# RWKV chunk: scaled k and b stored dense and multiplied by quadrants; one idle product in each of the first eight steps of the prompt's attention

## What is computed

```python
s = jnp.einsum('bhtr,bsr->bhts', q_lat, c) + jnp.einsum('bhtp,bsp->bhts', q_rope, kr)
p = jax.nn.softmax(masked(s * SOFTMAX_SCALE), axis=-1)
return jnp.einsum('bhts,bsr->bthr', p, c)
```

```python
sa = jnp.einsum('bhij,bhj->bhi', S, -kk_t)
S = S * w_t[:, :, None, :] + sa[..., None] * (kk_t * a_t)[:, :, None, :] + v_t[..., None] * k_t[:, :, None, :]
y_t = jnp.einsum('bhij,bhj->bhi', S, r_t)
```

## Time and profile before

| | |
|---|---|
| Median of 3 runs | 2264.63 us |
| The profiled execution's own time | 2272.78 us |
| Its span, first to last instruction | 2271.1 us |
| Mean granted TensorE clock over the span | 0.935 |
| PE busy | 2048.6 us (90%), 21448 matmul records |
| VectorE busy | 926.2 us (41%) |
| ScalarE busy | 642.5 us (28%) |
| GpSimd busy | 125.1 us (6%) |

### The profile page before, as it was taken

How to read it: one execution, slowest core, us unless ns; L and a number is a source line. 1 busy time by engine, 2 the same in 40 slices (tenths; PEclk the granted TensorE clock), 3 DMA queues, 4 the chain that set the end, 5 groups by cost and what they waited for, 6 DMA issues and landing times. The chain is left out here.

```text
span 2271.1 us, 50033 instructions
## 1 busy us (share of the span) xinstructions
PE 2048.6 (90%) x21448; PEld 1828.2 (81%) x21448; DVE 926.2 (41%) x1521; ACT 642.5 (28%) x1057; POOL 125.1 (6%) x167
## 2 busy tenths in 40 slices
PE   4789889998999999994899889999998989999995
PEld 3656556776889999994799669899853989999995
DVE  5323442222253333335942275454434353333334
ACT  2122334443142212222532323232211142212222
POOL 0001000431000000000000020000131000000000
PEclk7888799999999999996999999999986999999998
DMA  4012400774123232221122000001030122232321
GB/s 122 19 50 87 118 0 2 247 242 146 56 75 88 78 94 83 88 70 43 47 75 84 19 2 3 3 3 40 3 100 19 56 75 83 84 94 76 95 70 40
DMA packets 229236, 158.00 MB, mean 70 GB/s; under 512 B 12504, under 2 KB 221247, under 8 KB 228928
## 3 DMA queue, kind: packets, MB, share of 16 engines
q1 hardware_dynamic: 223412, 136.93, 20.3%
q0 software_dynamic: 5376, 18.36, 2.6%
q10 hardware_dynamic: 268, 0.08, 0.0%
HBM read 149.96 MB, written 5.34 MB: 68 GB/s over the span
## 5 line engine op out<-in xcount | busy, mean ns | idle before, releaser
L311 PE MATMUL ps<-ffn_xh,ffn_wh 128*128 128x280 f32 x1408 | 298.1, 293 | 18.0 <-DVE ffn_xl L1358 13.7
L311 PE MATMUL ps<-ffn_xh,ffn_wl 128*128 128x280 f32 x1408 | 299.3, 294 | 0.0
L311 PE MATMUL ps<-ffn_xl,ffn_wh 128*128 128x280 f32 x1408 | 296.6, 292 | 0.0
L311 PEld LDWEIGHTS ps<-ffn_xh,ffn_wh 128*128 128x128 f32 x1408 | 226.3, 190 | 19.0 <-issue 18.8
L311 PEld LDWEIGHTS ps<-ffn_xh,ffn_wl 128*128 128x128 f32 x1408 | 226.7, 191 | 0.0
L311 PEld LDWEIGHTS ps<-ffn_xl,ffn_wh 128*128 128x128 f32 x1408 | 224.2, 190 | 0.0
L1260 ACT CAST ffn_wh<-wa 128x1024 fp32r<-128x1024 f32 x88 | 91.3, 1041 | 208.8 <-PE ps L311 181.2
L311 PE MATMUL ps<-ffn_hid_h,ffn_wl 128*128 128x280 f32 x704 | 148.3, 292 | 0.0
L311 PE MATMUL ps<-ffn_hid_h,ffn_wh 128*128 128x280 f32 x704 | 147.6, 291 | 0.0
L311 PE MATMUL ps<-ffn_hid_l,ffn_wh 128*128 128x280 f32 x704 | 147.6, 291 | 0.0
L317 DVE TENSOR_TENSOR ffn_wl<-wa,ffn_wh 128x1024 fp32r<-128x1024 f32 x88 | 107.6, 1225 | 87.5 <-ACT ffn_wh L1260 87.5
(11 more groups left out here) (360 smaller groups left out, 3709.8 us busy)
## 6 DMA issues: line engine op xcount, KB each, us to landing
wa<-in_ffn_w_gate SPq DMA_DIRECT2D x44, 512.0 KB, 3.7
wa<-in_ffn_w_up SPq DMA_DIRECT2D x44, 512.0 KB, 3.7
arena<-in_cache SPq DMA_DIRECT2D x77, 160.0 KB, 3.4
wb<-in_ffn_w_down SPq DMA_DIRECT2D x16, 768.0 KB, 4.7
wb<-in_ffn_w_down SPq DMA_DIRECT2D x16, 640.0 KB, 4.4
arena<-in_cache POOLq DMA_DIRECT2D x63, 160.0 KB, 3.7
wb<-in_cache SPq DMA_DIRECT2D x40, 160.0 KB, 3.4
wb<-in_cache POOLq DMA_DIRECT2D x28, 160.0 KB, 3.6
```

The lines of the kernel that those rows point to most:

```text
L311: mm = nc.tensor.matmul(dst[:, s, 0:HALF], a[:, c * width:(c + 1) * width], b[:, c, s * HALF:(s + 1) * HALF], start=first and n == 0, stop ...
```

## The change

In `turn_and_mix`, steps with g = 0 get one idle product of 384 columns (identity times constants, into PSUM bank 7, read by nobody) between the turning product and the wait for ScalarE's copy. In the RWKV chunks `bnd`, `knd` and `bn` go; `bd` and `kd` hold b and k dense, 64 columns a pair. `scale` becomes two products of 128 partitions. ab, ak and the turning of k and b go by quadrants; the function `both` is gone. The clearing of the block-diagonal buffers ahead of the first chunk goes, and that of the last chunk shrinks. Four buffers of the last chunk that lay on top of `knd` and `bnd` get partly new places. All of it is in `last_tensor` too.

```diff
@@ turn_and_mix
             mm.then_inc(turned, 1)
+            if g == 0:
+                idle_products(pe, 1, 7, 3 * P)
             ge(pe, turned_kept, i + 1)
@@ buffers
-        bnd, knd = room(NP * 2 * L), room(NP * 2 * L)
+        bd, kd = room(NP * L), room(NP * L)
-        lw, cum, winv, fresh, vc, bn = (room(NP * L) for _ in range(6))
+        lw, cum, winv, fresh, vc = (room(NP * L) for _ in range(5))
@@ chunk_tensor, and the same in last_tensor
-            for b, src in ((0, knd), (7, bnd), (6, vc)):
+            for b, src in ((0, kd), (7, bd), (6, vc)):
...
                 for c in range(NP):
-                    if src is not vc:
-                        mm = nc.tensor.matmul(ps[:, b, c * L:(c + 1) * L], src[:, c], eye, start=True, stop=True)
-                        continue
                     for h in range(2):
                         rows = slice(RH * h, RH * h + RH)
                         mm = nc.tensor.matmul(ps[rows, b, c * L:(c + 1) * L], src[rows, c], eye[rows], start=True, stop=True)
...
-                both("ab", g, bnd, ar).then_inc(made["ab"], 1)
+                heads("ab", g, 2 * L, [(lo(bd), whole(ar))]).then_inc(made["ab"], 1)
...
-                heads("nab", g, L, [(lo(ar), lo(bn))]).then_inc(made["nab"], 1)
+                heads("nab", g, L, [(lo(ar), lo(bd))]).then_inc(made["nab"], 1)
...
-                both("ak", g, knd, ar).then_inc(made["ak"], 1)
+                heads("ak", g, 2 * L, [(lo(kd), whole(ar))]).then_inc(made["ak"], 1)
@@ scale
-                for x in (bnd, knd):
+                for x in (bd, kd):
                     nc.vector.memset(x, 0.0).then_inc(fresh_s, 1)
...
-            for dst, src in ((bnd, bv), (knd, k)):
-                for h in range(2):
-                    rows = slice(RH * h, RH * h + RH)
-                    op = nc.vector.tensor_tensor(dst[rows, :, L * h:L * h + n], src[rows, :, at], winv[rows, :, 0:n], ALU.mult)
-            op.then_inc(bk_scaled, 1)
-
-            if n < L:
-                nc.vector.memset(bn, 0.0).then_inc(fresh_s, 1)
-                dve.wait_ge(fresh_s, 4)
-            nc.vector.tensor_tensor(bn[:, :, 0:n], bv[:, :, at], winv[:, :, 0:n], ALU.mult).then_inc(bk_scaled, 1)
+            for dst, src in ((bd, bv), (kd, k)):
+                nc.vector.tensor_tensor(dst[:, :, 0:n], src[:, :, at], winv[:, :, 0:n], ALU.mult).then_inc(bk_scaled, 1)
@@ start of the chunks
-                nc.vector.memset(bnd, 0.0).then_inc(opened0, 1)
-                nc.vector.memset(knd, 0.0).then_inc(opened0, 1)
```

More of the change, by code:

```diff
@@ L1714, in program @@
         by_run = lambda x: x.rearrange("p (b i) -> p b i", b=DB)
-        v_own = [room(DB * L, DB), room(DB * L, DB), by_run(flat(mid)), by_run(flat(far))]
-        v_own += [by_run(flat(x)[:, n * DB * L:(n + 1) * DB * L]) for x in (knd, bnd) for n in range(2)]
+        v_own = [room(DB * L, DB) for _ in range(4)] + [by_run(flat(x)) for x in (mid, far, kd, bd)]
         sa_own = [by_run(flat(cum)), by_run(flat(winv))]
@@ L1761, in heads @@
             return mm
[L1763 to L1770, removed]
+        lo, hi, whole = lambda x: (x, 0, L), lambda x: (x, L, 2 * L), lambda x: (x, 0, 2 * L)
         def chunk_tensor(pe, i):
@@ L2025, in chunk_vector @@
                 nc.vector.memset(ar, 0.0).then_inc(fresh_s, 1)
-                dve.wait_ge(fresh_s, 5)
+                dve.wait_ge(fresh_s, 4)
             dve.wait_ge(grown, i * 2 + 1)
@@ L2177, in _ @@
                 nc.vector.memset(st, 0.0).then_inc(opened0, 1)
-                nc.vector.memset(bnd, 0.0).then_inc(opened0, 1)
-                nc.vector.memset(knd, 0.0).then_inc(opened0, 1)
                 nc.vector.memset(wc[:, :, 0:1], 1.0).then_inc(opened0, 1)
-                dve.wait_ge(opened0, 5)
+                dve.wait_ge(opened0, 3)
                 nc.vector.memset(fresh[:, :, 0:1], 0.0).then_inc(opened0, 1)
-                dve.wait_ge(opened0, 6)
+                dve.wait_ge(opened0, 4)
                 decay(dve, 0, L)
```

## The result

The changed kernel takes 2232.31 us (median of 4 runs, 2231.13 to 2234.50) against 2264.86 before on the same chip: ratio 0.9856, interval 0.9841 to 0.9870, 32.6 us less. The forecast was 2229 us, in a range of 2217 to 2243.

The account below looks back on a forecast made before the run. PE was taken to bound the chunks and attention steps; chunk terms of 26.6 us plus attention's 8.8 made 35.4, so 2264.6 - 35.4 = 2229.2 us, given as 2229, range 2217 to 2243.

Parts of the forecast that it names:

- Turning, ab and ak: Chunk front: turning k and b by quadrants gains 1.7 us; ab and ak take 1.75 us each, gaining 0.2 each.
- The quadrants pair: Rival: 128-column quadrant halves do not run side by side in the chunks, giving 2260 or 2317 us; chance 0.03.
- p2's front: Each chunk reaches p2 2.2 us sooner (2.0 to 2.4), 17.6 us over eight chunks.
- The last chunk: VectorE clears and makes ar first, hiding part of the front's gain: 1.1 us, between nothing and 2.2.
- t32 and the clock behind it: Chunks: shorter `scale` and clearing remove 6.9 of 7.1 us of PE waits for the m32 sum; clock fall, 1.5 us.
- More records to fetch: Chunks: 64 more matmul records each, 8% more to fetch, cost 0.5 us.
- The first chunk: VectorE's savings ahead of it give nothing, hidden by PE's ten idle products; cutting those would give some 4 us.
- The idle products: Attention: clock rises within eight steps, likely after two or three; +1.8, -5.3, and -5.3 for g = 1: -8.8 us.
- The bound of 2.5 us a step: Attention, g = 0: below some 2.5 us a step VectorE, not PE, would be the bound.
- 2243 fell: Rival: attention's clock does not rise in the eight steps, costing 4.8 us and giving 2243 us; chance 0.09.
- the masks did not make p2 late: Rival: VectorE's masks make p2 wait, so the front gives 8 instead of 17.6 us; with its alternative, chance 0.06.
- t32 waited for what the profile named: Rival: in the chunks t32 waits for something other than `scale`, so only 27 us come, 2237.6 us; chance 0.02.

Follow-up runs that it names:

- e2: The kernel before with only the idle product in the attention steps of g = 0 added: 2257.51 us.
- e1: The changed kernel without the idle product in attention, the RWKV chunks as changed: 2239.54 us.
- e3: The changed kernel with VectorE's `scale` as long as before (four half products, one more into an unread buffer): 2235.01 us.
- e6: The kernel of e3 with two more full products into spare buffers ahead of `scale`: 2249.01 us.
- e9: The kernel of e4 with the load of the samples' 2 MB state held back from chunk 6 to the last chunk: 2224.82 us.
- e4: The changed kernel with five idle products ahead of the first chunk instead of ten: 2226.15 us.
- e7: The changed kernel with attention's idle products of 128 columns instead of 384: 2239.56 us.
- e8: The kernel of e4 with idle products added ahead of the first scores (384 columns) and in step 0 (512): 2226.94 us.
- e10: The kernel of e4 again, unedited, on the same chip as e9: 2225.54 us.

## Why the prediction was right, and where its terms were off

**Turning, ab and ak.** k and b in 1.89 us against 2.0, ab, nab and ak in 4.43 against 1.75 + 1.75 and 1.0 for nab (1.08 before, less 0.08): as worked out. The quadrants pair: 64 records of 128 columns one after the other would alone have needed 64 x 0.107 = 6.8 us, an estimate from the earlier trace rows. The Trainium skill, TensorEngine Tiling (Array Packing), section Restrictions and Gotchas, says that different row tiles cannot access the same PSUM bank simultaneously. The two halves of these products write different partitions of one bank, and they ran side by side, so the trace does not agree.

**p2's front.** Mis-sized by a little: 9.82 to 7.26 is 2.56 us a chunk, 20.5 in eight, just above the top of 2.0 to 2.4. In chunk 2 turning k and b gave 1.82 us where 1.7 was put, v 0.15 where 0.08, and ab, nab and ak 0.61 where 0.48. VectorE's masks moved forward with ab and nab, as argued, and were again just in time.

**The last chunk.** 1.1 us was put, and 1.6 came: from its first turning product to x it took 18.02 us before and 16.45 after, although PE now waits up to 1.0 us for ar, by the row of L2064. In the stage's time it does not show: later in that chunk the clock falls in every trace, and in that of after it stayed low for longer. The stretches, of before and then of after:

```profile
1648.60:1665.70 17.10, 17.10 (x270) 14.65 (x268) 0.76 (x2) 0.64 (x2) 0.00 (x0) 0.50 0.05 17
```
```profile
1603.20:1623.60 20.40, 20.40 (x316) 17.30 (x314) 1.69 (x4) 0.64 (x2) 0.11 (x1) 0.50 0.05 16
```

The chunk as a whole so took 67.95 and 67.99 us. In e2 and e1, both with the longer low stretch, it took 69.59 and 68.05, the 1.5 apart. What decides between the two lengths is open.

**t32 and the clock behind it.** The 7.1 us of waits went whole, predicted 6.9, and with them the fall at 1601. That this is `scale`'s length is shown by e3 and e6; in e6 falls of the clock came back with the waits. With `scale` as long as before 4.4 us of waits come back in six, not 7.1: before, 4.0 of the 7.1 were in six waits and 3.1 in chunk 7's, which is 1.2 in e3. The other 1.9 of that wait went with the smaller clearing, as the prediction has it, but no run tests the clearing alone. e3's eight chunks take 258.83 us in its profile against 250.24 and 251.04 in those of the changed kernel, some 8 more: the 4.4, and 1.7 to 2.6 of pauses named issue (8.8 against 6.2 and 7.1). The medians differ by only 2.7 to 4.5; e3's profiled execution is the slowest of its four, and the changed kernel's profiled ones are the fastest of theirs, so the two profiles overstate the difference.

**More records to fetch.** Predicted 0.5 us. PE's own pauses named issue went from 3.6 to 6.2 us, 2.6 more, five times the term; in the other traces with dense chunks they are 5.3 to 9.6, in e2 with the old chunks 3.3. The prediction let PE's idle time grow by 8%, with the number of records; these pauses grew by half and more. e9 shows that such a pause can hang on a transfer beside it. The profiles' sum is 20.5 + 7.1 + 1.5 (the fall at 1601) - 2.6, with nothing for the last chunk as a whole, = 26.5 against 28.0 measured in the stage and 25.9 in the medians of e1; 1.5 us of the stage are not accounted for. The 26.6 predicted thus came out by errors that cancel: 2.9 more from the front, 2.1 less by the pauses, 1.1 less in the last chunk.

**The first chunk.** Nothing, as predicted, and the 4 us named as there to be taken were taken by e4.

**The idle products.** -8.8 predicted, -8.0 by e2, from errors that cancel. The clock rose after one slow step, not two or three: that step took 3.90 us (210.41 to 214.31) against 3.56, +0.34 in place of 1.8. Between the two traces steps 1 to 5 then save 6.5 us, steps 6 and 7, which took 4.84 each before and not 3.56, another 4.0, and the steps of g = 1 up to 252 some 4.4: 14.3 in all, with the first scores 0.2 longer. The bound of 2.5 us a step was read from VectorE's 2.64 us from mask to end of staging in one step with a pause in it; the same operations take 2.45 after (214.41 to 216.86), with the next mask starting right at its end, and steps 1 to 5 go below the bound. All this makes the gain larger. But the sum took the late rise of the clock, at 252, for what the runs do. e1 and e7 show kernels without a sufficient idle product at full clock from 236.5 and 234.5, with an attention of 154 us, and against that the gain is 7.4, all of it in the first eight steps (28.98 us in e1, 21.04 after): the 5.3 us put for g = 1 give nothing there. That the unprofiled runs of before rose now early, now late is argued from the 8 us between its profile and its median and from their mean clocks (31 executions beside the experiments: 0.933 to 0.940, 16 of them 0.938 or more, the profiled one 0.935), not shown. So the size was partly luck; that the clock rises within the eight steps was right.

**The rivals.** The clock rose, so 2243 fell; the masks did not make p2 late; the quadrants pair; t32 waited for what the profile named.

## What to carry to other kernels

Two products on quadrants can take less time than one on the whole array when half of the whole one multiplies zeros (1.89 us against 3.71 for turning k and b); the price was there in the trace, in the kernel's own wider quadrants. When work goes from one engine, look what another engine did beside it to fill time or keep its clock up: the idle products that once hid VectorE's work became the path, and halving them was worth another 4 us. A gain worked out from one profile of a stage whose clock rises late in some executions is that execution's gain; compare with a second profile, or test that part alone.

## What the runs showed that was not expected

- A PE that is busy for 27.23 of 27.30 us by its records can stay at 0.50 (e7's profile), while with 384 columns in the same place the clock rose to 1.00 some 7 to 8 us after the stage's first score in every profile but e8's, where it was up already.
- A 2 MB load, 9.5 us from issue to landing, went with a stop of PE for 2.1 us that is not there without it, in a stage where PE reads nothing from that load (e9 against e10). In the changed kernel's trace it landed in the same chunk, which took 33.73 us.
- Every pause of PE over 0.5 us named issue in the chunks, in all twelve traces, ended 2.2 to 2.9 us after an instruction transfer started.
